# Turning the results of the up and conv-input matmuls with VectorE's 32x32 transposes and a trip through device memory, in a two-layer decoder trunk

## What is computed

```python
def short_conv_mixer(h, w_in, conv_w, conv_b, w_out):
    bcu = h @ w_in
    b_gate, c_gate, u = jnp.split(bcu, 3, axis=-1)
    gated = c_gate * u
    y = lax.conv_general_dilated(
        gated, conv_w[:, None, :].astype(gated.dtype),
        window_strides=(1,), padding=[(CONV_WIDTH - 1, 0)],
...
    return (b_gate * y) @ w_out

def sq_relu_mlp(h, w1, b1, w2, b2):
    return jnp.square(jax.nn.relu(h @ w1 + b1)) @ w2 + b2
...
        h = x * (1.0 + sc_m) + sh_m
        if i % N_MIXERS == 0:
            j = i // N_MIXERS
            y = stick_breaking_attention(h, attn_w_qkv[j], attn_w_o[j])
        else:
            j = i // N_MIXERS
            y = short_conv_mixer(h, conv_w_in[j], conv_w[j], conv_b[j], conv_w_out[j])
        x = layer_norm(DEEPNORM_ALPHA * x + (1.0 + g_m) * y, ln_g[i, 0], ln_b[i, 0])
        h = x * (1.0 + sc_f) + sh_f
        y = sq_relu_mlp(h, mlp_w1[i], mlp_b1[i], mlp_w2[i], mlp_b2[i])
        x = layer_norm(DEEPNORM_ALPHA * x + (1.0 + g_f) * y, ln_g[i, 1], ln_b[i, 1])
```

## Time and profile before

| | us |
|---|---|
| median of three runs | 2266.32 |
| lowest and highest run | 2265.54, 2266.53 |
| span of the profiled execution | 2263.0 |
| TensorE busy in it | 2228.7 |
| VectorE busy | 1686.1 |
| ScalarE busy | 1180.4 |

### The profile page before, as it was taken

One profiled execution on the slowest core, in us unless ns is written; L12 is line 12 of the kernel. 1 busy time (PEld: TensorE's weight loads), 2 busy tenths in 40 slices (PEclk: granted clock), 3 DMA queues, 4 the chain that ended last, 5 costly groups with the idle time before them and its releaser, 6 DMA issues.

```text
span 2263.0 us, 28130 instructions
## 1 busy us (share of the span) xinstructions
PE 2228.7 (98%) x10886; PEld 1880.6 (83%) x10886; DVE 1686.1 (75%) x1690; ACT 1180.4 (52%) x1517; POOL 7.7 (0%) x25
## 2 busy tenths in 40 slices
PE   6999999999999999999999999999999999999998
PEld 5999987888888888888888888888888888888886
DVE  7899999986777777778778788878665555555567
ACT  4777784565355345445464444437634544543642
POOL 0000000000000000000000000000000000000000
PEclk9999999999999999999999999999999999999999
DMA  9999998799888888888859778876877667666662
GB/s 353 388 387 397 398 365 310 242 331 326 300 292 277 289 298 284 284 309 273 270 180 371 268 279 306 308 230 218 287 234 235 225 226 241 212 188 189 192 223 103
DMA packets 281525, 627.09 MB, mean 277 GB/s; under 512 B 19233, under 2 KB 27953, under 8 KB 279345
## 3 DMA queue, kind: packets, MB, share of 16 engines
q1 hardware_dynamic: 278432, 608.25, 78.4%
q10 hardware_dynamic: 2960, 17.05, 1.9%
HBM read 623.12 MB, written 2.10 MB: 276 GB/s over the span
## 4 chain that ended last, share of the span: by engine, by line
PE 93%; DVE 4%; issue 1%; DMA 1%; ACT 1%; SPq 0%; DVEq 0%; ACTq 0%
PE bank L1300 27%; PE bank L1302 27%; PE bank L1301 27%; PE bank L1290 3%; PE bank L1293 3%; PE bank L1292 3%; PE bank L1310 2%; DVE mod_acc L910 1%; PE bank L1328 1%; DMA raw<-in_attn_w_qkv 0%; DVE w_low L954 0%; DMA res<-in_x 0%; PE bank L1347 0%; PE bank L1372 0%; PE bank L1360 0%
## 5 line engine op out<-in xcount | busy, mean ns | idle before, releaser
L628 ACT ACTIVATE w_high<-raw 128x1024 fp32r<-128x1024 f32 x752 | 791.4, 1058 | 971.3 <-PE bank L1302 946.2
L954 DVE TENSOR_TENSOR w_low<-raw,w_high 128x1024 fp32r<-128x1024 f32 x752 | 915.8, 1223 | 501.7 <-ACT w_high L628 500.8
L1300 PE MATMUL bank<-w_high,h_high 128*128 128x512 f32 x1632 | 640.1, 392 | 2.9 <-DVE w_low L954 2.9
L1302 PE MATMUL bank<-w_high,h_low 128*128 128x512 f32 x1632 | 635.4, 389 | 0.0
L1301 PE MATMUL bank<-w_low,h_high 128*128 128x512 f32 x1632 | 635.3, 389 | 0.0
L910 DVE SCALAR_TENSOR_TENSOR mod_acc<-mod_raw,cond,mod_acc 128x1024 f32<-128x1024 f32 x345 | 442.1, 1281 | 27.2 <-DMA mod_raw<-in_mod_w 22.8
L1300 PE MATMUL bank<-w_high,hid_high 128*128 128x512 f32 x1120 | 437.2, 390 | 0.0
L1302 PE MATMUL bank<-w_high,hid_low 128*128 128x512 f32 x1120 | 435.8, 389 | 0.0
L1301 PE MATMUL bank<-w_low,hid_high 128*128 128x512 f32 x1120 | 435.8, 389 | 0.0
L1300 PEld LDWEIGHTS bank<-w_high,h_high 128*128 128x128 f32 x1632 | 306.5, 188 | 66.7 <-issue 3.6
L1302 PEld LDWEIGHTS bank<-w_high,h_low 128*128 128x128 f32 x1632 | 306.3, 188 | 64.2
(11 more groups left out here) (151 smaller groups left out, 1165.7 us busy)
## 6 DMA issues: line engine op xcount, KB each, us to landing
raw<-in_mlp_w SPq DMA_DIRECT2D x512, 512.0 KB, 4.5
mod_raw<-in_mod_w SPq DMA_DIRECT2D x368, 512.0 KB, 6.8
raw<-in_attn_w_qkv SPq DMA_DIRECT2D x96, 512.0 KB, 10.6
raw<-in_conv_w_in SPq DMA_DIRECT2D x96, 512.0 KB, 5.5
raw<-in_attn_w_o SPq DMA_DIRECT2D x32, 512.0 KB, 7.2
raw<-in_conv_w_out SPq DMA_DIRECT2D x32, 512.0 KB, 4.7
mod_raw<-in_mod_w SPq DMA_DIRECT2D x32, 256.0 KB, 6.6
gate_row<-in_mod_b ACTq DMA_DIRECT2D x4, 1024.0 KB, 7.5
```

Of the source, the lines that this page charges most:

```text
L628: act.activation(chunk_slots(n)[0], raw[:, n % NCH], ACT.Copy).then_inc(high_done, 1)
L954: dve.tensor_tensor(low_, raw[:, n % NCH], high.bitcast(F32), ALU.subtract).then_inc(raw_used, 1)
L1300: pe.matmul(dst, high[:, k, c], wh, start=first, stop=False, skip_group_check=True)
L1302: return pe.matmul(dst, low[:, k, c], wh, start=False, stop=last, skip_group_check=True)
```

## The change

TensorE no longer turns. Behind a unit's group, VectorE transposes both banks in blocks of 32x32 (`turn_quads`), with the columns taken at a stride of four: block (m, c) holds the columns m * 128 + 4 s + c for s = 0 to 31. A 32x32 transpose stays within 32 partitions, so a token quarter's features lie on 32 partitions, for each of four c. SyncE stores `stage[:, 0]` to a scratch tensor in device memory, `quads_out` (512 KB), and ScalarE's queue loads it back to `stage[:, 1]` with partition 4 s + c taking its four token quarters, in pieces of 1 KB (`read_quads`). Bias, ReLU and square then run in place there, and the writes of `hid_high`, `hid_low` and `y` reorder the columns (`by_quads`).

ScalarE's `copy_rows` is gone. The load back stands behind the high split of chunk 4, the `late` part behind that of chunk 5 instead of 4; VectorE's `late` part stands behind the low split of chunk 6 instead of 5. For the first four conv units ScalarE copies; for the other eight VectorE waits for the load itself. In the cut diff `swap_quads` is SyncE's, `read_quads` and the next two pieces are ScalarE's, `turn_quads` (called at the end of each unit's group) and `turned_conv` are VectorE's, and `turn` was TensorE's:

```diff
-    TURN_AFTER = 0
+    UNIT_GROUPS = ([W_MLP[0] + f * 2 * NG + g for f in range(FC) for g in range(NG)]
+                   + [W_CIN + i for i in range(3 * NG)]
+                   + [W_MLP[1] + f * 2 * NG + g for f in range(FC) for g in range(NG)])
...
+            def swap_quads(u):
+                i = u - U_CIN
+                if 0 < i <= NG:
+                    sp_.wait_ge(y_copied, i)
+                else:
+                    sp_.wait_ge(post_done, CREDIT_STAGE + (u if i <= 0 else u - NG))
+                sp_.wait_ge(banks_free, UNIT_GROUPS[u] + BANK0 + CREDIT_BANKS + 1)
+                sp_.dma_start(quads_out[:, :], flat(stage[:, 0])).then_inc(quads_saved, 16)
+
+            swap_at = {(w + 1) * NCH + SLOTS - 1 + NCH: u for u, w in enumerate(UNIT_GROUPS)}
             for n in range(N_HEADS + 2 * AHEAD, N_CHUNKS):
                 load_chunk(n)
+                if n in swap_at:
+                    swap_quads(swap_at[n])
...
+            def read_quads(u):
+                act.wait_ge(quads_saved, 16 * (u + 1))
+                act.dma_start(feat_quads, quads_out[:, :].rearrange("(a p) (c n) -> (p c) a n", a=QUADS, c=QUADS)
+                              ).then_inc(swapped, 16)
...
                 for j in range(first, NCH):
                     high(w * NCH + j)
-                    if late and j == SLOTS:
+                    if j == SLOTS and w - 1 in UNIT_GROUPS:
+                        read_quads(UNIT_GROUPS.index(w - 1))
+                    if late and j == SLOTS + 1:
                         late()
...
-                act.wait_ge(rows_turned, f * NG + U_MLP[layer] + g + 1)
-                act.wait_ge(post_done, f * NG + CREDIT_STAGE + S_MLP[layer] + g)
+                act.wait_ge(swapped, SWAP_DMAS * (f * NG + U_MLP[layer] + g + 1))
                 b1 = V_B1 + layer * (FF // P)
                 for m in range(GT):
                     at = f * KT + g * GT + b1 + m
-                    ins = act.activation(feat[:, m, :], bank[2 * (g % 2) + m // 2][:, T * (m % 2):T * (m % 2 + 1)],
-                                         ACT.Relu, bias=vec[:, at:at + 1])
-                ins.then_inc(banks_free, 1)
+                    ins = act.activation(feat_of(m), feat_of(m), ACT.Relu, bias=vec[:, at:at + 1])
+                ins.then_inc(lifted, 1)
...
+            def turn_quads(u):
+                w = UNIT_GROUPS[u]
+                if u:
+                    dve.wait_ge(swapped, SWAP_DMAS * u)
+                dve.wait_ge(chunk_mult, w * NCH + CREDIT_SPLIT + NCH)
+                for t in range(TT):
+                    ins = dve.transpose(turned_quads.rearrange("p c (m t s) -> p t m c s", m=GT, t=TT)[:, t],
+                                        bank[2 * (u % 2) + t][:, :].rearrange("p (m s c) -> p m c s", m=GT, c=QUADS))
+                ins.then_inc(banks_free, 1)
...
             def turned_conv(i):
-                dve.wait_ge(banks_free, w + BANK0 + CREDIT_BANKS + 1)
+                dve.wait_ge(swapped, SWAP_DMAS * (U_CIN + i + 1))
...
-            def turn(u, par, rows):
-                pe.wait_ge(rows_done, u + 1)
-                for m in range(GT):
-                    for t in range(TT):
-                        at = T * (m % 2) + P * t
-                        ins = pe.transpose(bank[2 * par + m // 2][:, at:at + P], rows[:, t, m * P:(m + 1) * P],
-                                           ident[:])
-                ins.then_inc(rows_turned, 1)
```

104 lines of the change are left out of this document (51 added, 53 removed).

## The result

| | before | after |
|---|---|---|
| median, us | 2265.99 | 2518.04 |
| lowest and highest run | 2265.54, 2266.53 | 2513.89, 2525.25 |
| ratio with 95% interval | | 1.1114 (1.1097 to 1.1132) |
| span of the profiled execution | 2263.0 | 2516.6 |

The change makes the kernel 252 us slower. The direction was forecast; the size is three times the +86 of the sum, and the time lies 88 us above the end of the range.

The account below looks back on a forecast made before the run. TensorE was taken to bound the kernel. New waits of 60 + 18 + 14 + 19 + 13 = 124 us, less 38, gave +86 on 2263.0; with 3.3 carried over, 2352 us. Range 2262 to 2430.

Parts of the forecast that it names:

- TensorE's turn: TensorE's 44 units of eight transposes go, at 0.87 us each: 38 us off the bound.
- Transposes at 1.28 us a pair: VectorE's two strided 128x512 transposes out of PSUM per unit, behind chunk 3's low split, take 1.28 us together.
- The rival of a dear strided read: VectorE's strided transposes take 2.56 us per turn or more: 36 to 51 us more, 2395 us; chance 0.15.
- Where ScalarE stops: ScalarE's work behind the load back delays chunk 6: ready 5.94 us (3.64 + 2.3) after the data is back.
- What hangs on the steps: Residual pass in three groups and gather in each MLP's last up run lengthen the loop: 19 and 13 us.
- The transfers, 8.4 and 7.2 us: Store plus load back per unit: 4.2 + 4.2 in first MLP and conv, 3.6 + 3.6 in second MLP.
- The rival of slow transfers: Store and load take 4.9 to 5.3 us each in place of 4.2: 75 us more, 2427; chance 0.15.
- its sum of +28: Store and load back at the skill's estimated 6.4 us for both: +28 us in all, 2294.
- VectorE's part of the loop, 9.84 us: First MLP, chunk 6's low split to the next turn: hidden units' low split, five chunks' low splits, 2.5 tiles.
- The clock: TensorE's granted clock was read as full before the change; the sum has no term for a fall.
- Conv: Conv input: 14 us of waits (copied units nothing, convolved 10, last four 4), plus 6.5 for the residual pass.
- The second MLP: Waits of 0.4 to 0.8 us, 1.2 for fourth units: 18 us, since the 21.9 loop is no longer than the group.

Follow-up runs that it names:

- the kernel with late places: Changed kernel with the load back issued by SyncE and ScalarE's and VectorE's work behind it moved later, mostly into the next group: 2319.29 us, ratio 1.0234 against before.
- thinner tiles: Modulation tiles from the fifth block on loaded at an eighth of their bytes: 2460.73 us in the changed kernel, 2229.68 with store and load left out.
- filler matmuls: Changed kernel with 14 unneeded matmuls into an unused bank ahead of chunk 6 of each group that follows a unit: 2505.64 us, ratio 1.1053 against before.

## Why the prediction was right in direction and wrong in size

- **TensorE's turn, -38 us: right.** 36.6 us of busy time and 32.7 of end time without the trip.
- **Transposes at 1.28 us a pair: right.** 1.31 in the timeline. The rival of a dear strided read falls. The Trainium skill (SBUF — State Buffer, the note on cachelines) speaks of matmuls that slow down on access that isn't contiguous; VectorE's reads at a stride of four show nothing of the kind, at 0.69 us against 0.68 for the adds of the same size that read a bank contiguously (L1176 before, L1203 after).
- **Where ScalarE stops, 5.94 us from data back to the low split of chunk 6: right.** 6.09 in the unit shown, 6.1 in the mean of six.
- **What hangs on the steps: near in the first MLP, too low for the residual pass elsewhere.** In the first MLP the run with the gather took 7.5 us more than the two plain runs (123.5 against 116.0; forecast 6.9). That with the residual took 12.1 more, of which 3.7 lie in its first group, ahead of any residual operation; 8.4 are left, forecast 6.8. In the second MLP the gather cost 3.2, forecast 6, but the run with the residual took 13.7 more than the plain ones (121.6 against 107.9), forecast 6; in conv the two groups with it lost 15.5 us, the two plain ones behind them nothing.
- **The transfers, 8.4 and 7.2 us: the term that was mis-sized.** The prediction's reason was that "during the load back ScalarE is blocked and few other loads start". That holds for the load: 4.0 against 4.2. The store was put at 4.2 as well, with the bytes ahead of it in the queue. It took 5.7 in the first MLP's units, 5.5 in the second's (forecast 3.6), up to 8.8 in conv. That bytes stand ahead of a store on this queue was known when it was priced, and weight loads on the same queue had a median of 5.3; 4.2 was below that. In the plain runs this is 2.0 of the 2.9 us that each loop took too long. The rival of slow transfers named it, with 9.8 to 10.6 for both, no less than the medians measured (5.7 + 4.0 in the first MLP), and still its sum was 2427, 91 us too low.
- **The coupling of stalls and landings: missing from the sum, and the smaller part.** The forecast added a fixed landing to a fixed loop. But a stall of ScalarE stops the low splits, these hold back the weight loads (three in 16 us), and when it ends they and the tiles go at once, so that more can stand ahead of the next store. The windows show the swings. Their price is bounded by the kernel with late places: with most stalls gone the store's landing falls by 0.5 us in the mean in each MLP, against 1.5 and 1.9 by which it exceeded the forecast there. Most of the excess is traffic that flows without stalls too. What the runs do show is that the landing takes up what VectorE gains or loses in front of it, and that thinner tiles give 57 us back with the trip and 4 without.
- **A transfer that meets few others.** By the Trainium skill (DMA: Bandwidth & Descriptors, the fit of fixed and variable cost, made with transfers issued by GpSimd) a transfer of 512 KB takes an estimated 3.2 us. The shortest store took 2.9 and the shortest load back 3.6, so the fit is near for a transfer that meets few others; it says nothing of one that does, and its sum of +28 was farther off than the forecast's +86.
- **VectorE's part of the loop, 9.84 us: too short.** 10.8 in the mean of six. In the unit shown it is 11.59, with three tiles for the forecast's 2.5 and the two sums of L933, left out of the count. By the kernel with more work on VectorE such a us comes to the end by less than a fifth, so little of the 166 us went here.
- **The clock: a term put at nothing.** It was taken as full; it fell to 0.958, and 99 of the 291 us of new waits and clock are matmuls at the lower level. By the filler matmuls the clock's worth is 12 to 52 us; the rest of the 99 is no loss of its own, since TensorE would idle instead.
- **Conv: 62 us, forecast 20.** By the same distances, with the gain added, the four groups behind the copied units lost 19 us (forecast nothing, and 6.5 for the residual pass), the four behind the convolved ones 27 (forecast 10), the last four 16 (forecast 4).
- **The second MLP: 98 us, forecast 30.** Here no loop through VectorE is needed. In 11 of the 16 units the turn is done 3.5 to 3.6 us after TensorE ends the group, as the forecast's first unit has it. With the landings measured, 5.5 + 3.8, chunk 6 is then ready at 3.5 + 9.3 + 6.1 = 18.9, 2.6 us late, where the forecast had 0.4 to 0.8. One case is a unit without a stall before it (store issued 2138.32, load issued 2141.99, low split of chunk 6 begun at 2151.32): its store took 3.6, and it made TensorE 1.7 us late; the store behind it took 6.0, behind weight loads that the stall had held back until 2154.84. In all TensorE is idle for 64 us there, and the other 34 are the lower clock, of which the filler gave 13 back.

So the step that failed is the price of the transfers, the store's above all, at 4.2 and 3.6 us where 5.7 and 5.5 were measured, and with it the clock that was put at nothing. Left open: how the 166 us beyond the forecast (57 in the first MLP, 42 in conv, 68 in the second) divide between landings, bursts, tiles and clock (some 54, the tiles' bytes, and 12 to 52, the clock, are measured, and they may overlap); and why ScalarE's stop in front of the load still costs 29 us when the work is late.

The signs that the prediction named came as said: L1310 gone, ScalarE's two waits in nearly every unit (38 and 36 of 44), TensorE's idle time on the low splits and on the first down group's hidden units. Its numbers were low: idle 226 for 160, the wait for the store 7.4 each for 4, a period of 28 to 29 for 25.5 in the first MLP and some 27 for 22.5 in the second. TensorE's busy time rose by 62 instead of falling by 40, which was the clock.

## What to carry to other kernels

A trip through device memory is priced by what stands behind its wait on every engine in program order, and not by its landing alone: 8.6 us of it were all but free for 20 units, while a similar trip cost 285 us for 44 where ScalarE stood in front of it. So move the consumer some chunks later before making the trip itself faster. Where the landing does count, take it from transfers that stand in the same loaded queue, at their median at least and with what is ahead of them, not from a value below that; the store here took 1.5 to 1.9 us more than it was given, at the median of each MLP. And work moved ahead of or behind such a transfer changes the time by far less than its own length, because the landing moves the other way.

## What the runs showed of the hardware

- A transpose in 32x32 blocks, fp32, of 128x512 out of PSUM on VectorE, with the columns taken at a stride of four, takes 0.69 us: as much as a contiguous add of that size out of PSUM (0.68).
- 512 KB from SBUF to device memory, between other traffic, in after: 2.9 us at least, 5.5 median, up to 8.8; 4.2 in the mean with at most two transfers ahead, 6.8 with four or more. The load back in pieces of 1 KB: 3.6 at least, 4.0 median.
- A store on ScalarE's queue, which carries little else, landed no sooner than on SyncE's (6.2 against 5.5).
- Of 211 us at half clock, two thirds could be regained by filler matmuls at a net gain of 12 us of time: the clock falls where TensorE waits, and 47 us or more of what the matmuls lose there would be waiting time anyway.
